# Block 1's inverse: a copy turned by 32x32 transposes on VectorE, flips and values behind p, and the next tile's rows ahead of the subtraction of p

## The reference, cut to what matters

```python
lower = jnp.where(strict, jnp.einsum('bnhid,bnhjd->bnhij', kb, kc) * decay, 0.0)
t_inv = lax.linalg.triangular_solve(eye + lower, eye, left_side=True, lower=True, unit_diagonal=True)
u = t_inv @ (vc * bc[..., None])
w = t_inv @ (kb * jnp.exp(gc)[..., None])
```

## Time and profile before

| what | value |
|---|---|
| runs before | 2091.72 us median of 3 (2091.34 to 2092.61) |
| the profiled execution | span 2090.9 us, from its first to its last instruction |
| what lies around the span, by the median | 0.8 us |
| TensorE busy | 1686.1 us, 81% of the span |
| VectorE busy | 623.6 us, 30% |
| ScalarE, GpSimd busy | 280.3 us and 105.4 us |
| chain that ended last | TensorE 46%, DMA 41%, VectorE 7% |

### The profile page before, as it was taken

One profiled execution on the slowest core, in us unless ns is written; L12 is line 12 of the kernel. 1 busy time (PEld: TensorE's weight loads), 2 busy tenths in 40 slices (PEclk: granted clock), 3 DMA queues, 4 the chain that ended last, 5 costly groups with the idle time before them and its releaser, 6 DMA issues.

```text
span 2090.9 us, 27267 instructions
## 1 busy us (share of the span) xinstructions
PE 1686.1 (81%) x10986; PEld 867.2 (41%) x10986; DVE 623.6 (30%) x1219; ACT 280.3 (13%) x588; POOL 105.4 (5%) x137
## 2 busy tenths in 40 slices
PE   6999989865666656666556666999999999999997
PEld 3677778411111111111111112888888433333332
DVE  3887664300000000000000001575613422222222
ACT  3213330200000000000000001213520100000001
POOL 0023321100000000000000001010200000000000
PEclk9999999988887887777888778999999999999999
DMA  9861014999999999999999999487357999999996
GB/s 401 358 244 76 3 61 162 382 429 430 432 431 431 431 431 431 431 431 429 431 433 431 431 431 396 161 308 281 107 175 297 397 426 427 427 427 427 427 428 280
DMA packets 55063, 730.56 MB, mean 349 GB/s; under 512 B 6145, under 2 KB 6593, under 8 KB 11330
## 3 DMA queue, kind: packets, MB, share of 16 engines
q1 hardware_dynamic: 52848, 722.23, 82.5%
q10 hardware_dynamic: 2130, 7.14, 1.0%
HBM read 728.26 MB, written 1.09 MB: 349 GB/s over the span
## 4 chain that ended last, share of the span: by engine, by line
PE 46%; DMA 41%; DVE 7%; issue 3%; ACT 1%; POOL 1%; DVEq 0%; SPq 0%; ACTq 0%; POOLq 0%
DMA ring<-in_w_moe 40%; PE psum L938 9%; PE psum L1144 7%; PE psum L979 5%; PE psum L613 4%; PE psum L959 2%; PE psum L631 2%; PE psum L1294 2%; PE psum L1306 1%; PE psum L1320 1%; PE psum L1843 1%; PE psum L913 1%; PE psum L1572 1%; PE psum L1457 1%; DVE ring L2691 1%
## 5 line engine op out<-in xcount | busy, mean ns | idle before, releaser
L613 PE MATMUL psum<-ring,main 128*32 128x512 f32 x2016 | 331.2, 818 | 189.8 <-DMA ring<-in_w_moe 184.4
L613 PEld LDWEIGHTS psum<-ring,main 128*32 128x32 f32 x2016 | 76.2, 143 | 435.1 <-DMA ring<-in_w_moe 231.7
L631 PE MATMUL psum<-ring,main 128*32 128x512 f32 x1000 | 145.7, 730 | 79.5 <-DMA ring<-in_w_moe 79.5
L673 DVE TENSOR_TENSOR main<-main,psum 128x512 f32<-128x512 f32 x16 | 11.0, 687 | 563.0 <-ACT main L694 563.0
L1144 PE MATMUL psum<-main,ring 128*128 128x256 f32 x768 | 167.6, 379 | 0.0
L938 PE MATMUL psum<-ring,main 128*64 128x512 f32 x688 | 153.8, 595 | 4.5 <-DMA ring<-in_w_moe 4.5
L1144 PEld LDWEIGHTS psum<-main,ring 128*128 128x128 f32 x768 | 145.4, 190 | 19.9 <-issue 0.5
L631 PEld LDWEIGHTS psum<-ring,main 128*32 128x32 f32 x1000 | 33.3, 126 | 175.9 <-DMA ring<-in_w_moe 108.9
L938 PEld LDWEIGHTS psum<-ring,main 128*64 128x64 f32 x688 | 48.6, 137 | 104.7 <-issue 93.4
L676 DVE TENSOR_TENSOR main<-psum,main 128x512 f32<-128x512 f32 x16 | 11.1, 692 | 242.6 <-PE psum L631 242.6
L694 ACT ACTIVATE main<-psum 128x512 f32<-128x512 f32 x16 | 9.6, 597 | 514.6 <-PE psum L613 514.6
(11 more groups left out here) (512 smaller groups left out, 2034.7 us busy)
## 6 DMA issues: line engine op xcount, KB each, us to landing
ring<-in_w_moe SPq DMA_DIRECT2D x70, 4096.0 KB, 23.6
ring<-in_w_moe SPq DMA_DIRECT2D x105, 2048.0 KB, 22.7
main<-in_w_moe SPq DMA_DIRECT2D x20, 2048.0 KB, 29.0
ring<-in_w_in SPq DMA_DIRECT2D x34, 1024.0 KB, 6.5
main<-in_w_moe SPq DMA_DIRECT2D x33, 1024.0 KB, 19.5
ring<-in_w_mod_t SPq DMA_DIRECT2D x24, 1024.0 KB, 6.6
main<-in_w_mod_t SPq DMA_DIRECT2D x16, 1024.0 KB, 8.0
ring<-in_w_moe SPq DMA_DIRECT2D x13, 1024.0 KB, 12.0
```

Of the source, the lines that this page charges most:

```text
L613: last = mm(psum[32 * j:32 * j + 32, b, :], xg1[:, k, :], w[:, 512 * j:512 * j + 512], start=k == 0, stop=k == KT - 1)
L631: last = mm(psum[q:q + 32, BANK_Y, :], hidT[:, P * (f % 4) + 32 * (f // 4):P * (f % 4) + 32 * (f // 4) + 32], w[:, r, 512 * g:512 * g + 51 ...
```

## The change

`begin_turn` leaves TensorE and ScalarE: VectorE transposes `inv` into `invT` itself, by one instruction that turns each 32x32 block in place. In levels 1 to 4, where the inverse is still made of blocks of at most 32, pd and its subtraction go, and VectorE transposes the new `invT` back into `inv` (`turn_blocks`) behind the subtraction of p. Level 5 keeps pd. On TensorE `fill_attention` (flips and values) moves from ahead of `solve_right` to behind it. On VectorE `decay_args` (levels 2 and 4 now, after levels 1 and 3 before), `lower_rows` and `query_rows` (levels 3 and 5 now) stand between `attend` and the subtraction of p, and for all tiles alike. `begin_turn` of tile t + 1 comes at the end of level 6 on VectorE, for tile 0 ahead of `side_sum(23)`. On ScalarE `decay_exps` moves behind `attend`. With the banks "lt" and most of "pd" gone, the banks are handed out in another turn.

```diff
@@ TensorE
             def solve_left(t, lv):
                 if lv == 1:
-                    pe.wait_ge(*banks.read_out(("lt", t)))
+                    pe.wait_ge(g_then_turned, 1 + TURNS * t + 1)
             def solve_right(t, lv):
-                if lv > 1:
-                    pe.wait_ge(*banks.read_out(("pd", t, lv - 1)))
+                if 1 < lv < LAST:
+                    pe.wait_ge(g_then_turned, 1 + TURNS * t + lv)
+                elif lv == LAST:
+                    pe.wait_ge(*banks.read_out(("pd", t, LAST - 1)))
...
                 last.then_inc(banks.when_full(("p", t, lv)), 1)
+                if lv < LAST - 1:
+                    return
                 o = banks.new(("pd", t, lv))
...
-                    fill_attention(n)
                     if n >= LATE_LEVELS:
                         fill_mods(n)
                     solve_right(t, lv)
+                    fill_attention(n)
...
-                        elif lv == LAST:
-                            begin_turn(t + 1)
@@ ScalarE
-            copy_begun(0)
...
+                    attend(n)
                     if t < 3 and lv in (2, 4):
                         decay_exps(t + 1, lv // 2 - 1)
-                    attend(n)
...
-                    if t < 3 and lv == LAST:
-                        copy_begun(t + 1)
@@ VectorE
+            def begin_turn(t):
+                dve.wait_ge(inverse_begun, 2 * t + 2)
+                turn_blocks(t)
+
+            def turn_blocks(t, back=False):
+                src, dst = (invT[t % 2], inv[t % 2]) if back else (inv[t % 2], invT[t % 2])
+                V.transpose(dst.rearrange("p d h n -> p (d h n)"), src.rearrange("p d h n -> p (d h n)")).then_inc(g_then_turned, 1)
...
+            begin_turn(0)
             side_sum(23)
...
                     attend(n)
-                    if t in LATE_TILES and lv in (3, 5):
+                    if t < 3 and lv in (2, 4):
+                        decay_args(t + 1, lv // 2 - 1)
+                    if t < 3 and lv in (3, 5):
                         lower_rows(t + 1, lv // 2 - 1)
+                        if t + 1 >= 2:
+                            query_rows(t + 1, lv // 2 - 1)
...
-                        dve.wait_ge(*banks.full(("pd", t, lv)))
-                        V.tensor_tensor(inv[t % 2], inv[t % 2], blocks(banks.tile(("pd", t, lv))), ALU.subtract).then_inc(banks.when_read(("pd", t, lv)), 1)
-                        dve.wait_ge(*banks.read_out(("pd", t, lv)))
+                        if lv < LAST - 1:
+                            turn_blocks(t, back=True)
+                        else:
+                            dve.wait_ge(*banks.full(("pd", t, lv)))
+                            V.tensor_tensor(inv[t % 2], inv[t % 2], blocks(banks.tile(("pd", t, lv))), ALU.subtract).then_inc(banks.when_read(("pd", t, lv)), 1)
+                            dve.wait_ge(*banks.read_out(("pd", t, lv)))
...
-                    if t < 3 and lv in (1, 3):
-                        decay_args(t + 1, lv // 2)
-                    if t < 3 and lv in (2, 4):
-                        if t not in LATE_TILES:
-                            lower_rows(t + 1, lv // 2 - 1)
-                        if t + 1 >= 2:
-                            query_rows(t + 1, lv // 2 - 1)
                     if t < 3:
                         recurrence(t, lv)
+                    if t < 3 and lv == LAST:
+                        begin_turn(t + 1)
```

More of the change, by code:

```diff
@@ L272, in build @@
         conv_silu = sem("conv_silu")
-        g_ready = sem("g_ready")
+        g_then_turned = sem("g_then_turned")
         kq_normed = sem("kq_normed")
@@ L558, in build @@
         LAST = 6
+        TURNS = LAST - 1
         ROW_OF = [2, 4, 3, 5]
@@ L1604, in _ @@
                     pe.wait_ge(consts_loaded, 16)
-                    pe.wait_ge(g_ready, 1)
+                    pe.wait_ge(g_then_turned, 1)
                     for d in range(2):
@@ L1743, in decay_rows @@
                 last.then_inc(banks.when_full(("gb", t, d)), 1)
[L1745 to L1753, removed]
             def solve_left(t, lv):
@@ L1891, in _ @@
             fourier()
-            begin_turn(0)
             n = 0
@@ L2265, in copy_keys @@
                     copy_out(("kk", t, par), kk_sb[:, par::2, :], lambda o: o[:, 0:2 * P].rearrange("p (c n) -> p c n", c=2))
-            def copy_begun(t):
-                copy_out(("lt", t), invT[t % 2], lambda o: o.rearrange("p (d h n) -> p d h n", d=2, h=H))
             for name in CHUNKS:
@@ L2808, in _ @@
             dve.wait_ge(dve_step, dve_steps())
-            dve.sem_inc(g_ready, 1)
+            dve.sem_inc(g_then_turned, 1)
             b2 = beta.rearrange("p t d h -> p (t d h)")
@@ L3018, in _ @@
                     dve.sem_inc(roped, 1)
+            begin_turn(0)
             side_sum(23)
             dve.sem_inc(mods_ready, 1)
-            LATE_TILES = (2,)
             def recurrence(t, lv):
```

## The result

The changed kernel takes 2106.85 us (median of 4 runs), the one before 2092.16: ratio 1.0055, 95% interval 1.0037 to 1.0072. It is slower by about 14.7 us, where 2.6 less were forecast, and lies outside the range. The profiled execution took 2105.89 us at a span of 2104.1, 13.2 more than before.

A forecast was written before the change was run, and what follows sets the result against it. The inverse was taken to bound the kernel, delaying mix_ready and the expert weight loads behind it. Terms −0.3 + 1.5 − 0.7 − 2.0 + 0.3 + 0.5 − 1.9 gave −2.6, so 2089.1 us, range 2085.5 to 2093.5.

The forecast's parts named there:

- T: Time of VectorE's new 32x32-block transpose over 128x512: taken as 0.69 us, an ordinary pass.
- Long T: Rival: the transpose takes 1.28 us, about +5.6, time 2094.7 us; chance 0.12, including a contended transpose.
- short T: Rival: the transpose takes 0.43 us, with full overlap 2086.7 us; chance 0.25, including a fuller overlap.
- Part 1: Start of tile 0: transpose ahead of side_sum(23) +0.69, pd gone from level 1 −1.0; net −0.3 us.
- Part 2: Tile 0, levels 2 to 5: rows ahead of p's subtraction make each level 6.06 to 6.09 us; net +1.5.
- Part 3: Tile 0, level 6: p ahead of flips and values, y to uw 4.3 us for 4.96; net −0.7.
- Part 4: Level 1 of tiles 1 and 2: pd leaves, −1.0 us each; tile 1 level 2, decay_args ahead: +0.3.
- Part 6: Tile 3, levels 1 and 2: pd no longer pushes recurrence work, −1.9 us together; levels 3 to 6 unchanged.
- Part 5: Differential-attention levels, tiles 1 and 2: rows fill exponential waits, but maxima and a query-row bank come late; net +0.5 us.
- off this path: Claim that ScalarE and GpSimd work does not lie on the inverse's critical path; no time was added for it.
- The clock rival: TensorE's clock halves in tile 0, y and scores double over four levels: +8.8, 2098 us; chance 0.05, shared with overlooked bank waits.
- The weights swallow it: Rival: expert weight stream does not hang on mix_ready, so no change shows: 2091.7 us; chance 0.03.

The follow-up runs named there:

- transposes_only: Kernel before with VectorE transposes replacing second products and their subtraction in levels 1 to 4; flips, values and rows in old places: 0.9997, median 2093.24 us.
- after_held: Changed kernel plus matmuls on constants in TensorE's waits between scores and p and behind some flips, written to a bank of their own: 1.0047.
- by_tile_3_held: Kernel before with transposes in tile 3 alone, plus 16 calls of matmuls on constants at the ends of tiles 0 to 2: 1.0011, median 2098.95 us.

## Why the prediction was wrong, step by step

*T.* Right: 0.69 forecast, 0.71 measured. The Trainium skill's pipelining of the transposing array (Vector Engine (DVE) Microarchitecture Reference, 3.8) agrees with it. The estimate of 1.24 from the Trainium skill's figure for 128x128 bf16 (VectorE: DVE Perf Modes, The three transpose paths) does not. Long T and short T both fall.

*Part 1*, start of tile 0: forecast −0.3, measured +0.1 (second y at 182.00, before 181.90).

*Part 2*, chain of 6.06 to 6.09 us a level in tile 0: right where the clock was 1.00. The level from 182.00 to 188.07 took 6.07, the one from 202.81 to 208.85 took 6.04. One of the four, from 188.07, took 8.7 at half clock, 2.6 more. Without it uw would have come at 210.5, 0.9 later than before where 0.5 was forecast.

*Part 3*, level 6: forecast 4.3, measured 4.26 (208.85 to 213.11).

*Part 4*: tile 1 level 1 forecast −1.0, measured −0.9 (216.32 to 222.69, 6.37); level 2 forecast 6.5, measured 6.53. Tile 2's level 1, forecast −1.0, took 9.38 us at half clock (266.77 to 276.15), where it was 7.31 before: +2.1.

*Part 6*, tile 3's first two levels: forecast −1.9, measured −1.7 (11.66 against 13.33).

*Part 5*, the levels with two score tiles: **here the sum failed**, with +0.5 forecast. From tile 1 level 5 to tile 2's uw the changed kernel took 74.5 us (243.53 to 317.99), the one before 60.2 (240.57 to 300.78): +14.3. Half of that is one level, tile 2 level 3, from y to y (283.31 to 298.59 above, and before):

```profile
273.63 1.15 PE L1767 MATMUL psum<-ring 64*64 64x64 f32 x32
...
281.97 1.15 PE L1767 MATMUL psum<-ring 64*64 64x64 f32 x32
```

It took 15.28 us where it was 8.34. TensorE waits 3.03 for the mask and 1.67 for the bank, where before it waited for neither; from the p at 288.54 to the next y its own products take 3.2 longer, at half clock, than at 1.00 (p 1.97 for 1.15, flips 1.12 for 0.66, values 1.81 for 1.00, decay_rows 2.02 for 1.16, the rest 0.3); and pd's 1.1 are gone. The sum had no such wait for the mask and no half clock. What it had was there: the wait for the exponentials fell from 2.1 to 1.0, and the late bank of the query rows was about as long as forecast (1.67 for 1.1). Not foreseen was that GpSimd's passes, moved with the decay arguments, meet the combination: "off this path" was wrong, though by itself cheap. The Trainium skill (SBUF — State Buffer, Who interferes with whom) has two-input passes contend with GpSimd's reads; this one has two inputs, and the trace agrees (1.64 to 1.81 us beside GpSimd, 0.75 alone). The prediction weighed that for T alone. Between the uw's of tiles 0 and 2 TensorE's idle time grew by 7.5 us, and the clock, which falls behind the waits and stays at half while TensorE has work, added up to 16 us of busy time. The sum priced the bank alone. How much of the 14.3 is the idle time and how much the clock is open, as the experiments say.

*The clock rival* is a good part of what happened, at a chance of 0.05 that it shared with an overlooked wait for a bank. Its price, 8.8, had the mechanism right (TensorE's own instructions take longer, y 1.95 for 1.15, if not the twice that it took) and the place wrong: tile 0 lost 2.6 to it, and in tiles 1 and 2 it made up to 16 us of busy time. The second step that failed, beside part 5, is its "against": a share of 5.74 of 8 us at clock 1.00 was taken to mean that such shares are safe. The changed kernel has 4.45 of 8 in that stretch, again at 1.00, and falls right behind it. A mean share says nothing of single waits, and the prediction's own chain of a level had lengthened TensorE's waits.

*The weights swallow it*: fell. The wait of SyncE is unchanged and 14.4 us at the experts' start show as 13.2 at the end.

## What to carry to other kernels

Taking work off TensorE gained 1.8 us in tile 0 here (transposes_only) and 2.8 in tile 3, and the kernel with transposes and flips still had no gain (1.0000) until matmuls on constants were put into six waits (0.9970). Before moving work ahead of a step on the chain, list the waits that it opens on TensorE, and price each twice: as idle time, and as a possible fall of the clock with the work behind it at half speed. A mean busy share does not show these waits, and not every wait is followed by a fall. Filling must go into the wait: behind p it delayed the next y. A bank of its own for the filling did no harm in the kernel with 0.9970, but in after_held p waited 3.77 us for one that the query products held.

## What the runs showed of the hardware that was not expected

The clock fell behind one stretch with TensorE busy 0.63 of 3 us and not behind another with 0.64 of 3, in the same execution. A wait of p of 2.26 us was followed by a fall in one kernel (by_tile_3_held) and not in another (the one before). A two-input pass of VectorE over 512 columns took 1.64 to 1.81 us beside two GpSimd passes, 0.75 alone. A 32x32 transpose over 128x512 f32 took 0.71 in main memory and in the ring alike, and also while GpSimd worked.
